# Lower part of x's second tile in the router stage: made by GpSimd behind the first tile's, instead of by VectorE behind the picks

## The reference, cut to what matters

```python
def hierarchical_moe(h, w_rg, b_rg, w_re, b_re, w_gate, w_up, w_down):
    """h: (N, D). Top-1 group, then top-2 experts inside that group; experts are SwiGLU MLPs."""
    ...
    g_logits = hf @ w_rg.astype(jnp.float32) + b_rg.astype(jnp.float32)
    ...
    _, g_idx = lax.top_k(g_logits, 1)
    ...
    top_v, top_i = lax.top_k(e_in_group, TOP_K_IN_GROUP)
    ...
    for g in range(N_GROUPS):
        ...
        act = jax.nn.silu(jnp.einsum('nd,edf->nef', h, w_gate[sl])) * jnp.einsum('nd,edf->nef', h, w_up[sl])
        act = act * combine[:, g, :, None]
        y = y + jnp.einsum('nef,efd->nd', act, w_down[sl])
    return y
```

## Time and profile before

| | us |
|---|---|
| median of 3 runs (688.09 to 688.76) | 688.09 |
| the profiled execution | 688.36 |
| its span in the trace | 686.5 |
| TensorE busy, matmuls | 637.4 (93%) |
| VectorE busy | 335.8 (49%) |
| ScalarE busy | 254.3 (37%) |
| GpSimd busy | 35.8 (5%) |
| mean DMA rate | 271 GB/s |

### The profile page before, as it was taken

How to read it: one execution, slowest core, us unless ns; L and a number is a source line. 1 busy time by engine, 2 the same in 40 slices (tenths; PEclk the granted TensorE clock), 3 DMA queues, 4 the chain that set the end, 5 groups by cost and what they waited for, 6 DMA issues and landing times.

```text
span 686.5 us, 10094 instructions
## 1 busy us (share of the span) xinstructions
PE 637.4 (93%) x4255; PEld 495.2 (72%) x4255; DVE 335.8 (49%) x409; ACT 254.3 (37%) x314; POOL 35.8 (5%) x25
## 2 busy tenths in 40 slices
PE   6999999999989988658868999999999999999995
PEld 5888999888856655335535588778888888888884
DVE  6856559656551121001111467678857444444436
ACT  6656563534411111000110454777234333433331
POOL 0010000000100000000000000742100000000002
PEclk9999999999999999957988999999999999999998
DMA  8979536688999999999999999335535555751001
GB/s 318 408 203 406 186 124 210 218 314 310 395 361 406 415 419 420 421 419 418 422 413 406 393 406 394 130 102 206 183 123 184 183 184 184 244 183 61 0 0 61
DMA packets 96358, 185.98 MB, mean 271 GB/s; under 512 B 9664, under 2 KB 33600, under 8 KB 96320
## 3 DMA queue, kind: packets, MB, share of 16 engines
q1 hardware_dynamic: 96032, 185.36, 72.0%
q10 hardware_dynamic: 288, 0.07, 0.0%
HBM read 184.37 MB, written 1.05 MB: 270 GB/s over the span
## 4 chain that ended last, share of the span: by engine, by line
PE 84%; DMA 8%; DVE 4%; issue 2%; ACT 1%; SPq 1%; POOL 0%; DVEq 0%; ACTq 0%
PE ps L721 20%; PE ps L723 20%; PE ps L722 20%; DMA ring<-in_w_down_e 5%; PE ps L977 4%; PE ps L1051 3%; PE ps L1006 3%; PE ps L1084 3%; PE ps L1072 2%; PE ps L1021 2%; DMA ring<-in_w_up_e 2%; DMA ring<-in_w_in 1%; PE ps L1372 1%; DVE heT L2267 1%; SPq L530 1%
## 5 line engine op out<-in xcount | busy, mean ns | idle before, releaser
L1481 ACT ACTIVATE w_hi<-ring 128x2048 fp32r<-128x2048 f32 (+1 forms) x65 | 117.1, 1828 | 12.6 <-PE ps L723 7.5
L1947 DVE TENSOR_TENSOR w_lo<-ring,w_hi 128x2048 fp32r<-128x2048 f32 x43 | 97.8, 2286 | 22.5 <-ACT w_hi L1481 22.3
L722 PE MATMUL ps<-w_lo,xT_hi 128*128 128x512 f32 (+1 forms) x272 | 102.6, 377 | 0.0
L721 PE MATMUL ps<-w_hi,xT_hi 128*128 128x512 f32 x240 | 96.0, 400 | 0.5 <-DVE xT_lo L2362 0.3
L723 PE MATMUL ps<-w_hi,xT_lo 128*128 128x512 f32 x240 | 93.7, 391 | 0.0
L722 PEld LDWEIGHTS ps<-w_lo,xT_hi 128*128 128x128 f32 x272 | 51.3, 189 | 8.7
L721 PEld LDWEIGHTS ps<-w_hi,xT_hi 128*128 128x128 f32 x240 | 45.1, 188 | 10.8 <-issue 0.8
L723 PEld LDWEIGHTS ps<-w_hi,xT_lo 128*128 128x128 f32 x240 | 45.0, 188 | 9.8
L721 PE MATMUL ps<-w_hi,hR_hi 128*128 128x512 f32 x112 | 44.3, 395 | 0.2 <-DVE w_lo L1979 0.2
L723 PE MATMUL ps<-w_hi,hR_lo 128*128 128x512 f32 x112 | 43.6, 390 | 0.0
L722 PE MATMUL ps<-w_lo,hR_hi 128*128 128x512 f32 x112 | 43.6, 389 | 0.0
(11 more groups left out here) (349 smaller groups left out, 1195.7 us busy)
## 6 DMA issues: line engine op xcount, KB each, us to landing
ring<-in_w_in SPq DMA_DIRECT2D x28, 1024.0 KB, 13.4
ring<-in_w_up_e SPq DMA_DIRECT2D x28, 1024.0 KB, 14.6
ring<-in_w_gate_e SPq DMA_DIRECT2D x27, 1024.0 KB, 12.2
ring<-in_w_down_e SPq DMA_DIRECT2D x24, 1024.0 KB, 17.8
ring<-in_w_gate SPq DMA_DIRECT2D x11, 1024.0 KB, 5.2
ring<-in_w_up SPq DMA_DIRECT2D x11, 1024.0 KB, 7.4
ring<-in_w_down SPq DMA_DIRECT2D x11, 1024.0 KB, 5.0
ring<-in_w_out SPq DMA_DIRECT2D x8, 1024.0 KB, 9.8
```

What stands on the lines that cost most here:

```text
L721: mm(o, a_hi, b_hi, start=start, stop=False, skip_group_check=True)
L722: mm(o, a_hi, b_lo, start=False, stop=False, skip_group_check=True)
L1481: return nc.scalar.activation(o, i, ACT.Copy)
L1947: tt(w_lo[slot][:], ring[:, slot, :], f32(upper_of(i)), ALU.subtract).then_inc(lo_made, 1)
```

## The change

VectorE no longer makes `xs_lo1a` and `xs_lo1b`, nor waits for `xshi_made` and `xslo_made` there. GpSimd makes them right after `xs_lo0`, as soon as ScalarE has made the second tile's upper part, and counts up `xslo_made` behind each half as VectorE did. TensorE's waits and SP's are unchanged.

```diff
@@ -2284,11 +2284,6 @@
 
             dve.wait_ge(place_made, 2)
             slots(0, start0, 1)
-            dve.wait_ge(xshi_made, T)
-            dve.wait_ge(xslo_made, 1)
-            for dst, ks in ((xs_lo1a, slice(0, KD // 2)), (xs_lo1b, slice(KD // 2, KD))):
-                x = X[:, 1, :].rearrange("p (q k) -> p k q", k=KD)
-                tt(dst[:], x[:, ks, :], f32(xs_hi[:, 1, ks, :]), ALU.subtract).then_inc(xslo_made, 1)
 
             step(tt(emask, oh2, egrp, ALU.mult))
             ts(oh1, rank, 0.0, None, ALU.is_equal)
@@ -2654,10 +2649,10 @@
                 pool.wait_ge(xshi_made, t + 1)
                 x = X[:, t, :].rearrange("p (q k) -> p k q", k=KD)
                 for dst, ks in parts:
-                    ins = tt(dst[:], x[:, ks, :], xs_hi[:, t, ks, :].bitcast(F32), ALU.subtract)
-                ins.then_inc(xslo_made, 1)
+                    tt(dst[:], x[:, ks, :], xs_hi[:, t, ks, :].bitcast(F32), ALU.subtract).then_inc(xslo_made, 1)
 
             xs_lower(0, ((xs_lo0, slice(0, KD)),))
+            xs_lower(1, ((xs_lo1a, slice(0, KD // 2)), (xs_lo1b, slice(KD // 2, KD))))
 
             pool.wait_ge(zstat_made, 1)
             own = [0]
```

## The result

The changed kernel takes **694.38 us**, the median of eight runs (690.59 to 698.24), beside 688.44 us for the kernel before in its eight (688.09 to 690.01): ratio 1.0079, 95% interval 1.0061 to 1.0097. Forecast were 689.9 us with a range up to 692.4: the direction was right, the size was not, and the time lies outside the range.

What follows compares the result with a forecast made beforehand. Bound: the routing chain into the gather, then full DMA. Gain 0, picks 2.3 us late, of which 1.8 reaches the end: 688.36 + 1.8 = 690.2, less 0.27 for the median of the runs, 689.9 us; range 688.0 to 692.4.

Steps and rivals of the forecast that it cites:

- What bounded the kernel: Router stage: routing arithmetic and TensorE's matmuls up to the gather at 191.62 us, then full DMA that wins back no idle time.
- The gain of 0: Behind the picks: taking two subtractions, 2.1 us overlapped, off VectorE gives TensorE nothing; gain on the compute path 0.
- The wait of 2.3 us: Routing arithmetic: VectorE's operations with two SBUF inputs stand still beside GpSimd's halves, making picks and gather 2.3 us late.
- the middle case: Routing arithmetic: VectorE gets one or two 0.2 us operations in between GpSimd's halves; delay 2.65 less 0.2 to 0.6 us.
- Its lower end: Smallest delay of VectorE if it gets one or two operations in between GpSimd's halves, put at 2.05 us.
- `early_c` at +0.1: SP's load issued at 193.79 us stays where it was, +0.1, its seeding matmul now ending at about 193.9.
- so I take 2.3: Price of TensorE's clock falling to half after 2.9 us idle: at most 3.5 us of work lost, taken as 2.3.
- the rival in which it falls: TensorE's clock falls after the longer idle time; first load 4.6 us late, 691.8 us in all, chance 0.30.
- the same four fifths: Share of the first ring load's lateness taken to reach the end: 1.8 of 2.3 us, also used for the clock rival.
- the 1.8 us, four fifths of 2.3: Part of the 2.3 us lateness said to reach the end through the first ring load, since most DMA engines had run dry.
- The full-clock case: Main forecast: picks late by 2.0 to 2.7 us with TensorE's clock held, 689.9 us, chance 0.42.
- The prediction's lower bound: First ring load: 0 of the 2.3 us reaches the end, as the slowest DMA engine, some 2 us behind, hides it.

Runs made afterwards that it cites:

- e6: Kernel before, with VectorE forming the logits six times and 15 filling matmuls on TensorE ahead of its wait for the assignment; 689.29 us, ratio 1.000.
- e1: Changed kernel, with 15 small bf16 matmuls (results thrown away) on TensorE ahead of its wait for the assignment; 690.34 us, ratio 1.0009.
- e5: Kernel before, with VectorE forming the logits six times to delay the assignment without GpSimd work beside it; 696.49 us, ratio 1.0061.
- e9: Changed kernel run again with nothing edited, on another chip; 693.61 us, ratio 1.006.
- e10: Kernel before, with SP's ring loads of the expert weights waiting for three finished TensorE units instead of one; 689.93 us, ratio 1.0006.
- e8: Changed kernel, with 7 filling matmuls on TensorE ahead of its wait for the assignment; 691.39 us, ratio 1.0025.
- e11: Kernel before, with SP's ring loads of the expert weights waiting for six finished TensorE units instead of one; 693.05 us, ratio 1.0053.
- e7: Changed kernel, but VectorE makes the first half behind the pick and GpSimd only the second, after it; 690.26 us, ratio 1.0005.
- e2: Changed kernel, but GpSimd waits for the first pick before making the second tile's two halves; 689.96 us, ratio 1.0009.

## Why the prediction was wrong

**What bounded the kernel** was read rightly in the main: the chain runs through the routing arithmetic into the gather, then the DMA engines are full, and a hole as large as that at 200 to 205 us in after is not won back. That no idle time ahead of the stretch is won back was too strong: e6 won back its 2.3 us, to within 0.8 us either way.

**The gain of 0** on the compute path was right: VectorE's freed time lies behind the picks, where it waits 5.07 us for the gather in after.

**The wait of 2.3 us** was right in mechanism, place and size (2.4). VectorE got its turn once between the halves, for one operation, and waited again for the second: the middle case. Its lower end was added up wrongly (one or two operations of 0.2 us take off 0.2 to 0.4 us, not 0.6, so 2.25 and not 2.05), which changed nothing. GpSimd's halves took 1.51 us each instead of 1.44.

**`early_c` at +0.1** holds only at full clock: +0.2 in e1, but 195.87 - 193.79 - 0.85 = +1.2 in after, where the seeding matmul ahead of it ran at half clock.

**Failed: "so I take 2.3", the price of the clock's fall, and its chance of 0.30.** These are the main failure: the forecast of 689.9 stands on a clock that holds, and even the rival in which it falls ended at 691.8. The price was shortened because TensorE "has more to do here than there, which brings it back sooner". It was not back sooner than the 6.9 us taken from the stretch at 350 us; the row of after shows the clock down for 16.6 us with TensorE busy for 16.17 of them:

```profile
193.60:210.20 16.60, 16.17 (x123) 11.03 (x127) 5.37 (x30) 1.69 (x3) 0.00 (x0) 0.51 0.64 228
```

From the mean of 0.76 over e5's stretch from 205 to 210 it lasted there to 205 + 0.24 x 5 / 0.5 = 207.4, 13.4 us behind the row of 193.96. So the way from the gather to the first ring load took 203.24 - 194.89 = 8.35 us instead of 196.23 - 191.62 = 4.61: 3.7 us more, where 2.3 were taken. With it and the wait of 2.4 us, at the same four fifths, the rival would have been 688.09 + 4.9 = 693.0. On TensorE itself the fall costs 7.0 us by the end of the first quad (9.4 late, less 2.4). As to the chance, the one row of before that showed a stall of this length was followed by the fall, and this was weighed down by "TensorE was waiting more often around that one". It fell in 15 of 20 executions of after and in 8 of 12 of e5. Since it falls in some executions only, the median goes with the more frequent case, and the rival should have been the forecast. The Trainium skill (TensorE: Matmul & The Clock Gate, HAM oscillation) says that waits for a load between stretches of matmuls throttle the clock again. The wait here is one for VectorE, and the profiles agree: half clock behind 2.99, 3.00 and 2.88 us of idle time (after, e9, e5), full clock behind 0.55 and 0.44 us (e1, e6).

**Failed: the 1.8 us, four fifths of 2.3, as what reaches the end.** The full-clock case lost 0.6 us (e1, -0.6 to 1.9) or nothing (e6, -0.8 to 0.8) instead of 1.8, so its own forecast, 689.9, was too high by about 1; e6 shows the end unmoved although the DMA share fell to 0.57 for 5 us, and e10 with 0.4 us (-0.4 to 1.2) agrees. e8 doesn't fit so well: 1.7 us (0.3 to 3.2), one fallen execution among them. The prediction's lower bound, that the slowest DMA engine hides the lateness, fits e6 and e10, but no row here shows which engine was last, so it stays argued. From e10 to e11 2.7 us more lateness of the first load (5.6 - 2.9) cost 3.3 us more, about all of it.

Put together for the executions with the fall: 2.4 (wait) + 3.7 (half clock) = 6.1 us late, of which e11 says that about 4 are lost. The medians of the slower groups lie 5.2 (e9), 6.4 (after) and 7.2 us (e5) above before. The difference from e11 lies at least in part in the loads behind the first, which the half clock delays again: the second group of ring loads (`ring<-in_w_up_e`) starts 9.4 us late in after and 2.3 in e11, and `early<-in_w_down_e` 6.3 against 3.6. What e5 loses beyond this, and why the clock stayed low for 13.4 to 16.6 us with TensorE nearly always busy, stays open.

## What to carry to other kernels

A wait put on an engine's path is priced twice: by its length, and by what it makes TensorE's clock do. Here a wait of 3.0 us where one of 0.6 stood brought half clock in about seven of ten executions, and behind the fall TensorE's way to the first load that it releases took 8.35 us instead of 4.61. Two-input operations and scales from SBUF to SBUF waited here until the GpSimd subtraction beside them ended, while a copy out of PSUM (184.60) and a reduction (e7) went through, so work moved to GpSimd belongs beside such operations, or where nobody waits for VectorE. How much of a load's lateness in front of a saturated stretch reaches the end is not a fixed share of the first load's: 2.3 to 2.9 us cost nothing that could be told in e6 and e10, 5.6 us cost 3.7. In the profiles it is read better from a load further back, which has already lost or kept the lateness.

## What the runs showed of the hardware that was not expected

- Behind an idle time of TensorE of 2.9 to 3.0 us ahead of small matmuls the clock was at 1.2 GHz in all three profiled executions of after, e9 and e5. By time and mean clock it fell in 23 of 32 executions of these kernels and held in the other nine; at 1.7 to 1.9 us it fell in 4 of 23. One kernel thus has two times, 688.5 to 691 and 695 to 699 us in e5, and nothing between.
- The low clock lasted 13.4 to 16.6 us of nearly gapless matmul rows.
- Fifteen bf16 matmuls of 128x384, 2.60 us of work whose result nobody reads, kept it at 2.4 GHz and took the loss away (e1, e6).
- Between two back-to-back GpSimd operations the waiting VectorE operation got through, and the next one that can be held up waited for the second: 1.34 and 1.44 us in after, 1.53 and 1.41 in e2.
- GpSimd's memsets did not hold up two-input operations, but did a VectorE scale from SBUF to SBUF: 0.51 us instead of 0.17.
- A VectorE reduction inside a GpSimd subtraction kept its 0.16 us (e7).
